# Moving x and the memory keys and values to DRAM and back in pieces, with the residual returning on the queue of the weight loads

## What is computed

```python
for layer in range(DEPTH):                       # DEPTH = 2
    x = x + rms_norm(mix, attn_norm_post)        # mix: attention of this layer
    f = conv_ffn(rms_norm(x, ffn_norm_pre[layer]), ffn_w_in[layer], ...)
    x = x + rms_norm(f, ffn_norm_post[layer])

def conv_ffn(h, w_in, conv_w, conv_b, w_out):    # w_in 2048 x 11264, w_out 5632 x 2048
    u = h @ w_in
    c = conv_b + sum(conv_w[j] * shifted(u, j) for j in range(3))
    g, val = c[..., :D_FF], c[..., D_FF:]
    return (gelu(g) * val) @ w_out
```

## Time and profile before

| | |
|---|---|
| median of 3 runs | 2188.17 us (2184.94 to 2188.7) |
| the profiled execution, its own time | 2188.01 us |
| its span in the trace | 2185.8 us |
| mean granted clock of PE in it | 0.994 of 2.4 GHz |
| PE busy | 2157.1 us, 99% |
| DVE, ACT busy | 1624.2 us (74%), 1249.0 us (57%) |
| moved by DMA | 416.68 MB, mean 191 GB/s |

### The profile page before, as it was taken

One profiled execution on the slowest core, in us unless ns is written; L12 is line 12 of the kernel. 1 busy time (PEld: TensorE's weight loads), 2 busy tenths in 40 slices (PEclk: granted clock), 3 DMA queues, 4 the chain that ended last, 5 costly groups with the idle time before them and its releaser, 6 DMA issues.

```text
span 2185.8 us, 32593 instructions
## 1 busy us (share of the span) xinstructions
PE 2157.1 (99%) x11589; PEld 1866.7 (85%) x11589; DVE 1624.2 (74%) x2280; ACT 1249.0 (57%) x1764; POOL 11.0 (1%) x28
## 2 busy tenths in 40 slices
PE   9999999999999999999899999999999999999997
PEld 8989988888888888888788889888888888888885
DVE  5757756677777767988779867567778776779786
ACT  5745745566555555655465567566565555555553
POOL 0000000000000000000000000000000000000000
PEclk9999999999999999999999999999999999999998
DMA  8555265565556565666656653655655555566664
GB/s 292 175 185 183 79 218 200 170 199 188 187 182 201 175 205 196 206 209 197 234 159 204 196 164 126 193 195 190 202 182 186 189 191 187 183 209 208 204 202 173
DMA packets 202664, 416.68 MB, mean 191 GB/s; under 512 B 13053, under 2 KB 13431, under 8 KB 201295
## 3 DMA queue, kind: packets, MB, share of 16 engines
q1 hardware_dynamic: 200687, 400.29, 56.6%
q0 software_dynamic: 1888, 15.21, 1.8%
HBM read 408.11 MB, written 7.34 MB: 190 GB/s over the span
## 4 chain that ended last, share of the span: by engine, by line
PE 96%; DVE 2%; DMA 1%; ACT 1%; issue 0%; DVEq 0%; POOL 0%; SPq 0%; ACTq 0%
PE ps L814 29%; PE ps L768 20%; PE ps L1308 20%; PE ps L822 15%; PE ps L852 4%; PE ps L862 3%; DMA w_raw<-in_ffn_w_out 1%; PE ps L1551 1%; PE ps L943 1%; PE ps L1454 0%; PE ps L1073 0%; DVE w_lo L2416 0%; PE ps L915 0%; PE ps L1008 0%; PE ps L1079 0%; PE ps L1104 0%
## 5 line engine op out<-in xcount | busy, mean ns | idle before, releaser
L2492 DVE TENSOR_TENSOR w_lo<-w_raw,w_hi 128x1024 fp32r<-128x1024 f32 x450 | 541.4, 1221 | 263.2 <-ACT w_hi L1771 259.1
L814 PE MATMUL ps<-xT,w_hi 128*128 128x512 f32 x2752 | 659.3, 391 | 0.0
L1771 ACT ACTIVATE w_hi<-w_raw 128x1024 fp32r<-128x1024 f32 (+1 forms) x466 | 476.9, 1040 | 230.8 <-PE ps L822 86.7
L814 PEld LDWEIGHTS ps<-xT,w_hi 128*128 128x128 f32 x2752 | 506.7, 189 | 98.7 <-issue 0.4
L822 PEld LDWEIGHTS ps<-xT,w_lo 128*128 128x128 f32 x2752 | 353.9, 192 | 18.6 <-DVE w_lo L2492 5.2
L822 PE MATMUL ps<-xT,w_lo 128*128 128x256 f32 x2752 | 359.0, 283 | 4.8 <-DVE w_lo L2492 4.8
L1308 PE MATMUL ps<-w_hi,hT_hi 128*128 128x512 f32 x576 | 227.4, 395 | 13.0 <-DVE w_lo L2416 11.8
L1308 PE MATMUL ps<-w_lo,hT_hi 128*128 128x512 f32 x576 | 226.5, 393 | 0.0
L1308 PE MATMUL ps<-w_hi,hT_lo 128*128 128x512 f32 x576 | 226.2, 393 | 0.0
L768 PE MATMUL ps<-w_hi,xT 128*128 128x512 f32 x640 | 203.2, 392 | 0.0
L2416 DVE TENSOR_TENSOR w_lo<-w_raw,w_hi 128x1024 fp32r<-128x1024 f32 x126 | 152.5, 1223 | 23.4 <-ACT w_hi L1725 16.3
(11 more groups left out here) (343 smaller groups left out, 2735.4 us busy)
## 6 DMA issues: line engine op xcount, KB each, us to landing
w_raw<-in_ffn_w_in SPq DMA_DIRECT2D x352, 512.0 KB, 4.1
w_raw<-in_ffn_w_out SPq DMA_DIRECT2D x176, 512.0 KB, 4.7
w_raw<-in_shared_w_kv SPq DMA_DIRECT2D x48, 512.0 KB, 4.4
w_raw<-in_a_w_o SPq DMA_DIRECT2D x32, 512.0 KB, 4.7
w_raw<-in_b_w_in SPq DMA_DIRECT2D x32, 512.0 KB, 4.6
w_raw<-in_b_w_o SPq DMA_DIRECT2D x32, 512.0 KB, 4.5
w_raw<-in_a_w_mem_kv SPq DMA_DIRECT2D x16, 512.0 KB, 6.0
w_raw<-in_b_w_mem_kv SPq DMA_DIRECT2D x16, 512.0 KB, 4.1
```

What stands on the lines that cost most here:

```text
L814: mm = nc.tensor.matmul(ps[:, base + m4, :].rearrange("p (a n) -> p a n", a=2), w_hi[:, slot, cols], xT[:, :, 2 * k + c, :], start=k == c ...
L1771: nc.scalar.activation(w_hi[:, s % R, 0:width], w_raw[:, s % R, 0:width], ACT.Copy)\
L2492: nc.vector.tensor_tensor(w_lo[:, s % R, :], w_raw[:, s % R, :], w_hi[:, s % R, :].bitcast(F32), ALU.subtract)\
```

## The change

The same data move to and from DRAM, in other pieces, at other times and partly on another queue, and the order of the entries of half 1 changes.

- `x_leaves`: x goes out in four pieces of 512 columns for both token halves (512 KB each), piece q after step s_in + 1 + 2q is used. The keys and values follow after IN0 + 9 and IN0 + 11.
- ACT waits for all of them inside its loop, ahead of the first `sums_hi`, and no longer ahead of the loop.
- `x` returns on SP in four pieces, each issued in `out_weights` behind one particular weight load (`X_RETURNS`, loads 58, 65, 73 and 81 of 88), after SP has waited for PE to have used the last unit that reads that quarter (entries 73, 85, 96 and 108).
- The keys and values return in SKV, on POOL, after steps SKV + 16 and SKV + 24.
- `TAILS` = (4, 8): four plain entries of tile 3 move in half 1 from the gaps between the units to behind `OUT_ENDS[2]`, which is 112 and no longer 116; the last unit is entries 105 to 108 and no longer 109 to 112.

```diff
-REST, TAIL = 3, 4
+REST, TAILS = 3, (4, 8)
-        between = first[LEADS[half]:-REST] + second[:-TAIL]
+        between = first[LEADS[half]:-REST] + second[:-TAILS[half]]
-        for step in second[-TAIL:]:
+        for step in second[-TAILS[half]:]:
+X_RETURNS = [next(r for r, raw in enumerate(OUT_RAWS) if raw[2] == "entry"
+                  and raw[3] >= [e for e in range(OUT_ENDS[1], OSTEPS)
+                                 if OUT_ENTRIES[e][0] == "even"][2 * q + 1] + R + 1)
+             for q in range(4)]
+PAIR_ENDS = [e + 1 for e in range(OUT_ENDS[1], OSTEPS) if OUT_ENTRIES[e][0] == "even"]
...
+                    if r in X_RETURNS:
+                        q = X_RETURNS.index(r)
+                        sp.wait_ge(step_used, s_out + PAIR_ENDS[2 * q + 1])
+                        sp.dma_start(x[:, :, 512 * q:512 * (q + 1)],
+                                     x_kept[:, :, 512 * q:512 * (q + 1)]).then_inc(x_back, 16)
...
-            def x_leaves(pieces):
-                pool.wait_ge(x_piece, pieces)
-                pool.dma_start(x_kept, x[:, :, :].rearrange("p t n -> p (t n)")).then_inc(x_spilled, 16)
-            def x_returns(s_out):
-                pool.wait_ge(step_used, s_out + UNIT_ENDS[1])
-                pool.dma_start(x[:, :, :].rearrange("p t n -> p (t n)"), x_kept).then_inc(x_back, 16)
+            def x_leaves(pieces, s_in):
+                for q in range(4):
+                    pool.wait_ge(x_piece, pieces)
+                    pool.wait_ge(step_used, s_in + 1 + 2 * q)
+                    pool.dma_start(x_kept[:, :, 512 * q:512 * (q + 1)],
+                                   x[:, :, 512 * q:512 * (q + 1)]).then_inc(x_spilled, 16)
...
             pool.wait_ge(kv_summed, 1)
+            pool.wait_ge(step_used, IN0 + 9)
             pool.dma_start(km_kept, kmT_b[:, :, :].rearrange("p h m -> p (h m)"))\
+            pool.wait_ge(step_used, IN0 + 11)
             pool.dma_start(vm_kept, vm_b[:, :, :, :].rearrange("p u h n -> p (u h n)"))\
-            x_returns(OUT0)
+            pool.wait_ge(step_used, SKV)
+            causal_rows(2)
+            pool.wait_ge(step_used, SKV + 2 * DSTEPS)
             pool.dma_start(kmT_b[:, :, :].rearrange("p h m -> p (h m)"), km_kept)\
+            pool.wait_ge(step_used, SKV + 3 * DSTEPS)
             pool.dma_start(vm_b[:, :, :, :].rearrange("p u h n -> p (u h n)"), vm_kept)\
...
                 def sums_hi(i):
+                    act.wait_ge(kv_spilled, 32)
+                    act.wait_ge(x_spilled, 64 * (layer + 1))
...
-                act.wait_ge(kv_spilled, 32)
-                act.wait_ge(x_spilled, 16 * (layer + 1))
                 for first, end in ((0, PAIRS // 2), (PAIRS // 2, FJ)):
```

More of the change, by code:

```diff
@@ L282, in program @@
         vm_kept = nc.dram_tensor("vm_kept", (P, MH * M), F32, kind="Internal").ap()
-        x_kept = nc.dram_tensor("x_kept", (P, TT * D), F32, kind="Internal").ap()
+        x_kept = nc.dram_tensor("x_kept", (P, TT, D), F32, kind="Internal").ap()
         y_f = at("y_f", [P, TT, D], F32, XT0)
@@ L687, in gain_rows_of @@
                 pool.dma_start(dst[:, :], vec[name].partition_broadcast(P)).then_inc(gain_landed, 16)
-            def x_leaves(pieces):
-                pool.wait_ge(x_piece, pieces)
-                pool.dma_start(x_kept, x[:, :, :].rearrange("p t n -> p (t n)")).then_inc(x_spilled, 16)
-            def x_returns(s_out):
-                pool.wait_ge(step_used, s_out + UNIT_ENDS[1])
-                pool.dma_start(x[:, :, :].rearrange("p t n -> p (t n)"), x_kept).then_inc(x_back, 16)
-            x_leaves(PIECES_IN0 + len(FFN_PIECES))
+            def x_leaves(pieces, s_in):
[4 more added lines that the diff above has]
+                                   x[:, :, 512 * q:512 * (q + 1)]).then_inc(x_spilled, 16)
+            x_leaves(PIECES_IN0 + len(FFN_PIECES), IN0)
             pool.wait_ge(kv_summed, 1)
+            pool.wait_ge(step_used, IN0 + 9)
             pool.dma_start(km_kept, kmT_b[:, :, :].rearrange("p h m -> p (h m)"))\
                 .then_inc(kv_spilled, 16)
+            pool.wait_ge(step_used, IN0 + 11)
             pool.dma_start(vm_kept, vm_b[:, :, :, :].rearrange("p u h n -> p (u h n)"))\
@@ L705, in _ @@
             gain_rows_of("ffn_post0", gain_f, OUT0)
-            x_returns(OUT0)
+            pool.wait_ge(step_used, SKV)
+            causal_rows(2)
+            pool.wait_ge(step_used, SKV + 2 * DSTEPS)
             pool.dma_start(kmT_b[:, :, :].rearrange("p h m -> p (h m)"), km_kept)\
                 .then_inc(kv_back, 16)
+            pool.wait_ge(step_used, SKV + 3 * DSTEPS)
             pool.dma_start(vm_b[:, :, :, :].rearrange("p u h n -> p (u h n)"), vm_kept)\
                 .then_inc(kv_back, 16)
-            pool.wait_ge(step_used, SKV)
-            causal_rows(2)
             gain_rows_of("b_post", gain_ob, OB)
-            x_leaves(PIECES_IN1 + len(LAST_PIECES))
+            x_leaves(PIECES_IN1 + len(LAST_PIECES), IN1)
             gain_rows_of("ffn_post1", gain_f, OUT1)
-            x_returns(OUT1)
         @blk.tensor
@@ L2927, in wide_epilogue @@
                 if folds is not None:
-                    dve.wait_ge(x_back, 16 * (folds // 4 + 1))
+                    dve.wait_ge(x_back, 64 * (folds // 4 + 1))
                 def last_tile(t):
```

## The result

The changed kernel takes 2162.49 us (median of 4 runs, 2161.15 to 2162.98) against 2187.01 us for the kernel before (2184.94 to 2188.7, 4 runs): a ratio of 0.9887, 95% interval 0.987 to 0.9904. The forecast was 2160.7 us, and a gain of 27.4 us; the medians are 24.5 us apart and the spans of the two profiled executions 25.0 us.

A forecast was written before the change was run, and what follows sets the result against it. PE was taken as the bound, so only its idle and the half clock behind pauses could be won: 7.3 + 9.8 + 9.1 + 1.2 = 27.4 us, giving 2160.7 us, with an 8-in-10 range of 2157 to 2170.

The forecast's parts named there:

- What bounds the kernel: Whole kernel: PE is busy 2157.1 of 2185.8 us, so only its 28.7 us idle and what hangs on them can be won.
- the seven waits: PE's waits for splits in IN0, OUT0 and OUT1, 17.8 us together, priced with the half clock behind them.
- Term 1: Start of IN0: ACT's wait for vm_kept moves to sums_hi, where it is covered; gain 7.3 us.
- Terms 2 and 3: Ends of OUT0 and OUT1: pauses for a late load and for entry 119's split go; gains 9.8 and 9.1 us.
- Term 4: Last unit's sums: two waits of 0.6 us go because the unit comes inside the fifth split slot's entries; gain 1.2 us.
- 512 KB instead of 3 MB competes with the last loads: Ends of OUT0 and OUT1: less returning data (2 MB before in OUT1) beside the last weight loads, so their pauses go.
- the margin of 1.8 us: End of OUT0: entry 119's split ready at T + 13.2, PE there at T + 15.0; before, short by 2.2 us.
- SP's waits: Half 1, four per layer before returning x: longest 5.5 us at the second, others 1 to 2.5; cost taken as 0.
- SP's wait starves the ring: Rival, 3%: SP's wait for step_used delays weight loads, eight waits costing 40 us; 2200 us, slower than before.
- The queue rule: Return of x on the weights' queue: each load behind a piece waits for all of it; uncovered, 10.6 us back, 2171.
- What the profile was to show: IN0 groups 5.57 us apart, clock 1.00 at OUT ends, PE's waits down some 17 us, busy time about 10.
- no wait for a weight load of more than 1 us: Sign for the ends of OUT0 and OUT1: no longer wait for a weight load behind entry 112.

The follow-up runs named there:

- run 4: The kernel before with only ACT's two waits for x, keys and values moved into sums_hi, transfers untouched: 2181.44 us.
- run 1: The kernel before with the new order of entries alone, x, keys and values whole on POOL as before: 2178.79 us.
- run 3: The changed kernel with the way out undone: x in one piece, keys and values right behind it, ACT's wait ahead of its loop: 2168.97 us.
- run 2: The changed kernel with the old order of entries, so the new transfers alone: 2174.24 us.
- run 5: The changed kernel with the last quarter of x issued behind load 87, the last weight load: 2160.3 us, and 2160.79 when repeated.
- run 8: The changed kernel with the four quarters of x returned on POOL's queue behind the same steps, SP not waiting: 2161.31 us.
- run 6: The changed kernel with keys and values fetched back early, on POOL after the last unit of OUT0, OUT1 untouched: 2165.12 us.
- run 7: The changed kernel with x returned whole, one 2 MB transfer on POOL after the last unit: 2169.34 us.
- run 11: The changed kernel with quarters 0 to 2 of x returned one load earlier and the last behind load 87: 2165.44 us.

## Why the prediction was right, and where it was off

- **What bounds the kernel.** Right: the gain is the seven waits (16.1 us less) and the half clock behind them (9.1 us less busy), together 25.2 us where the span is 25.0 shorter.
- **Term 1, IN0.** Right to 0.02 us, and for the reason given, the place of the wait (run 4). The pieces play no part in it. That it is so close is also luck: the old pause was 4.78 us in the profile of the forecast, 6.45 and 5.57 us in those of runs 1 and 3, where IN0 took 506.1 and 505.6 us.
- **Terms 2 and 3.** Two causes were named, the late load and the split behind the scaling. They are not separate: the split of the late load stands ahead of the second add, so a load that is late makes squares, scaling and the last splits late as well. The kernel before and run 2 have the same chain. The order alone gives 4.5 and 5.6 us, the transfers alone 3.9 and 6.0, in profiles of which the second was 3.2 us below its median.
- **Term 4.** Right: the two waits stay with the old order (run 2) and go with the new one (run 1).
- **The step that was mis-sized.** "512 KB instead of 3 MB competes with the last loads" was priced at 0, and the margin of 1.8 us was worked out with the second add at T. A quarter of x was taken for 1.3 us of DMA; ACT began on load 82 2.96 us later with it than without (run 5), and the add came at T + 3.9. Against run 5 that cost 1.1 us in OUT0 and 0.9 in OUT1 (the pauses of 0.79 and 0.59 us with what hangs on them). The rest of the 2.4 us missing is 0.43 us ahead of IN0, where the same code starts at 357.07 to 359.07 us in the profiles here.
- **The wrong entry.** The margin was worked out for entry 119, which did not hold PE. Entry 115 did, the first split behind the scaling. From the add to the start of its split the trace has 3.97 us, the split takes 1.22, and PE reaches the entry at T + 8.4: with the add at T there are 3.2 us to spare, with the add at T + 3.9 it is 0.8 short. (The forecast's 3.8 us ran from 1087.16, a row of PE; the add before began at 1087.02, and 3.97 us lie between it and that split too.)
- **SP's waits.** The second was forecast at 5.5 us and is 5.1 (4.9 in OUT1); the others were forecast at 1 to 2.5 us and are 0.3 to 1.5, 1.0 on average. Their price, taken as 0, is 0 in OUT0. The 0.3 us behind the second return in OUT1 are not shown to be theirs: that pause stands in run 8 too, where SP doesn't wait (0.26 us), and in only one of the two profiles of run 5's kernel. The rival "SP's wait starves the ring", 2200 us, is a real mechanism: two loads earlier it gives 2204, one load earlier 5 us, all at the second quarter.
- **The queue rule.** 10.6 us were to come back by it if nothing covered them. Moved to POOL's queue the same quarters give 2161.3 us, hardly to be told from the changed kernel's 2162.5. The queue of its own, which by that working was to be the milder for the weights, was not: load 82 needed 9.1 us there and 8.7 behind the quarter. Nor were the packets of x 2 KB there: between 1053 and 1064 us POOL's queue moved 0.52 MB in 144 packets, 3.6 KB each, SP's 2.23 MB in 1151, 1.9 KB each.
- **What the profile was to show.** Right: the groups of IN0, the clock of 1.00, 17 us less waiting (16.1) and 10 us less busy (9.1). Wrong: "no wait for a weight load of more than 1 us" behind entry 112; ACT waited 5.14 us, and 2.92 us for a later load.

The best version is run 5, one line away from the changed kernel. 512 KB cost 3 us and not 1.3. From 1053 to 1064 us the DMA engines moved 264 GB/s with 80% of their time taken; at that rate 512 KB are 2.0 us, an estimate that comes near the 2.28 us by which the way of load 82 grew, and the other 0.68 us are its later issue. Open is what kept the engines from the 396 GB/s of the earlier trace rows; no run tested it.

## What to carry to other kernels

When a pause follows a late load, look at what else stands behind that load's split on the same engine: the lateness is passed through the whole chain, and the first split behind the chain, not the last, is the one to work out a margin for. A bulk transfer beside a tight load cost about the same here on either queue; it was its time that had to move, not its queue. A wait on the queue that feeds the weights is free as long as the loads behind it have cover, and dear as soon as one has not: here one load (0.5 MB) more behind the wait cost 5 us and two cost 44.

## What the runs showed of the hardware that was not expected

A pause of PE of the same length is not always followed by half clock. Behind 2.04 us (run 6) the granted clock was 0.50, 1.2 GHz; behind 2.08 us at the same entry (run 7) it stayed at 1.00, 2.4 GHz, though PE had stood 0.32 us already 3 us ahead of that pause. Behind 1.79 us (run 11) it was 1.00 from 1024.5 to 1025.5 us and 0.50 from 1026.5 to 1028.5, with PE busy again throughout. What decides is not shown. The timeline row of the pause and the stretch behind it, of run 6:

```profile
1072.96 0.80 PE L1320 MATMUL ps<-w_hi,hT_hi 128*128 128x512 f32 x1 [2.04 <-DVE w_lo L2428]
```

```profile
1073.00:1075.00 2.00, 2.00 (x5) 1.62 (x6) 2.00 (x2) 1.03 (x2) 0.00 (x0) 0.50 0.38 93
```

and of run 7:

```profile
1072.70 0.50 PE L1321 MATMUL ps<-w_hi,hT_hi 128*128 128x512 f32 x1 [2.08 <-DVE w_lo L2429]
```

```profile
1073.00:1075.00 2.00, 2.00 (x10) 1.62 (x9) 2.00 (x3) 0.77 (x1) 0.00 (x0) 1.00 0.55 123
```

Against run 5's OUT0 the one pause of run 6 cost 4.4 us, the two of run 7 (2.4 us) 3.0, and the 0.79 us of the changed kernel 1.1. Between these runs and run 8 (0.47 us of pause, 1.1 us of length) a pause in OUT0 cost 1.2 to 2.3 times its length.
